# Low parts of the second FFN matrix by an accumulating DMA, in two groups of a hybrid Conformer / mLSTM step

## What is computed

```
h2 = _rmsnorm(x, g_fn)
gt, up = jnp.split(h2 @ w_fi, 2, axis=-1)
x = x + (jax.nn.silu(gt) * up) @ w_fo
```

## Time and profile before

| | us |
|---|---|
| two runs | 1012.42, 1013.75 |
| their median | 1013.09 |
| span of the profiled execution, first to last instruction | 1012.8 |
| TensorE busy in it | 978.7 |
| VectorE, ScalarE, GpSimd busy | 595.8, 382.2, 185.8 |

### The profile page before, as it was taken

How to read it: one execution, slowest core, us unless ns; L and a number is a source line. 1 busy time by engine, 2 the same in 40 slices (tenths; PEclk the granted TensorE clock), 3 DMA queues, 4 the chain that set the end, 5 groups by cost and what they waited for, 6 DMA issues and landing times.

```text
span 1012.8 us, 19204 instructions
## 1 busy us (share of the span) xinstructions
PE 978.7 (97%) x7178; PEld 957.5 (95%) x7178; DVE 595.8 (59%) x870; ACT 382.2 (38%) x511; POOL 185.8 (18%) x160
## 2 busy tenths in 40 slices
PE   6999989999999999999999999999999999999993
PEld 5999879999999999999999999999999999999993
DVE  6876768698597869875365553333333343333355
ACT  5643444345235434536533443331122221122242
POOL 4042051014005101400230022220022220022202
PEclk9989989999999999999999999999999999999997
DMA  6227403521521352142522222223222222222222
GB/s 188 79 63 147 105 22 116 188 83 42 218 84 42 124 177 83 42 139 81 177 84 76 85 86 81 77 77 99 83 72 88 89 86 83 83 82 78 66 64 93
DMA packets 29389, 96.96 MB, mean 96 GB/s; under 512 B 7296, under 2 KB 7440, under 8 KB 28320
## 3 DMA queue, kind: packets, MB, share of 16 engines
q1 hardware_dynamic: 27600, 78.01, 24.5%
q0 software_dynamic: 1744, 18.42, 5.8%
HBM read 84.03 MB, written 12.39 MB: 95 GB/s over the span
## 4 chain that ended last, share of the span: by engine, by line
PE 51%; issue 32%; DVE 5%; POOL 5%; ACT 4%; DMA 2%; POOLq 0%; SPq 0%; DVEq 0%; ACTq 0%
PE ps L892 38%; POOL hf L587 3%; PE ps L1137 3%; PE ps L992 2%; POOL hid_lo L589 2%; DMA raw<-w_head_in 2%; ACT hid_hi L869 2%; PE ps L1016 1%; PE ps L1064 1%; PE ps L1002 1%; DVE w_lo L1170 1%; PE ps L1073 1%; DVE rs L1185 1%; DVE hf L1232 1%; ACT w_hi L614 1%
## 5 line engine op out<-in xcount | busy, mean ns | idle before, releaser
L892 PE MATMUL ps<-h_hi,w_hi 128*128 128x288 f32 x1472 | 317.0, 297 | 1.4 <-DVE w_lo L1170 1.4
L892 PE MATMUL ps<-h_lo,w_hi 128*128 128x288 f32 x1472 | 314.4, 295 | 0.0
L892 PE MATMUL ps<-h_hi,w_lo 128*128 128x288 f32 x1472 | 314.4, 295 | 0.0
L614 ACT ACTIVATE w_hi<-raw 128x1024 fp32r<-128x1024 f32 x136 | 143.8, 1058 | 383.1 <-PE ps L892 370.6
L1170 DVE TENSOR_TENSOR w_lo<-raw,w_hi 128x1024 fp32r<-128x1024 f32 x136 | 191.4, 1408 | 160.2 <-ACT w_hi L614 159.5
L892 PEld LDWEIGHTS ps<-h_hi,w_hi 128*128 128x128 f32 x1472 | 236.1, 189 | 3.3 <-issue 2.6
L892 PEld LDWEIGHTS ps<-h_lo,w_hi 128*128 128x128 f32 x1472 | 237.0, 189 | 0.0
L892 PEld LDWEIGHTS ps<-h_hi,w_lo 128*128 128x128 f32 x1472 | 236.9, 189 | 0.0
L1385 DVE SCALAR_TENSOR_TENSOR conv<-a_p,vec,conv x120 | 96.8, 807 | 0.2
L587 POOL TENSOR_TENSOR hf<-hf,rs 128x576 f32<-128x576 f32 x22 | 31.4, 1426 | 347.8 <-DVE hf L1609 347.8
L1575 DVE TENSOR_TENSOR x<-ps,x 128x576 f32 (+1 forms) x32 | 24.3, 758 | 89.8 <-PE ps L892 89.8
(11 more groups left out here) (255 smaller groups left out, 1223.8 us busy)
## 6 DMA issues: line engine op xcount, KB each, us to landing
raw<-w_fi_in SPq DMA_DIRECT2D x44, 512.0 KB, 3.5
raw<-w_head_in SPq DMA_DIRECT2D x40, 512.0 KB, 3.5
cs<-st_c_in POOLq DMA_DIRECT2D x4, 2048.0 KB, 9.2
c_s_out<-cs POOLq DMA_DIRECT2D x4, 2048.0 KB, 7.7
raw<-w_fo_in SPq DMA_DIRECT2D x16, 512.0 KB, 3.5
x<-xT_in SPq DMA_DIRECT2D x16, 288.0 KB, 4.1
raw<-w_cgcv_in SPq DMA_DIRECT2D x8, 512.0 KB, 3.7
raw<-w_ga_in SPq DMA_DIRECT2D x8, 512.0 KB, 3.5
```

The costliest lines, as they stand in the source:

```text
L614: act.activation(w_hi[:, s, :], raw[:, s, :], ACT.Copy).then_inc(hi_ready, 1)
L892: last = pe.matmul(ps[:, 2 * s + b, 0:HALF], wt[:, w, k * P:k * P + P], src[:, k, b * HALF:b * HALF + HALF], start=(k == 0 and wt is w_hi ...
```

## The change

In groups 0 and 1 of the FFN, for the eight splits made in the loop of the second matrix, the subtraction on DVE goes. ACT writes the negated rounded weight into `w_lo[s]` right behind the rounded one (`-raw`, written as `F32R`, is rounded like `raw`). POOL then issues a DMA that adds the raw weight onto it, with `accum_op=ALU.add`, which leaves raw minus rounded. In group 0 the DMA reads the raw weight from the buffer `raw[s]` in SBUF, in group 1 from the weights in DRAM again. DVE waits until the DMA has landed (`lo_landed[s]`) and raises `lo_ready` itself, twice through the same order: first its own wait that the previous increments are there, then the increment. There are 16 such splits of the kernel's 136. All others stay as they were.

```diff
@@ gpsimd, behind the loop over hidden tiles of group g
+                def add_raw(at, s, of):
+
+                    pool.wait_ge(neg_ready, at + (s + 1))
+                    pool.dma_start(w_lo[:, s, :], of, accum_op=ALU.add).then_inc(lo_landed[s], 16)
+
+                for n in range(KT if g < 2 else 0):
+                    beyond = n + 2 - KT
+                    if g == 0:
+                        of = raw[:, n % 2, :]
+                    else:
+                        of = w_fo1[n + 2] if beyond < 0 else w_fi[2 * Q_E[2] + beyond]
+                    add_raw(g * KT + n - n % 2, n % 2, of)
@@ scalar, the loop of the second matrix
                             split_hi(i + (U_F[g] + 2) // 2, s)
+                            act.activation(w_lo[:, s, :], raw[:, s, :], ACT.Copy, scale=-1.0).then_inc(neg_ready, 1)
@@ vector, add_units
-                    if not last:
+                    if base in U_F[:2]:
+
+                        dve.wait_ge(lo_landed[s], i * 16 + (8 * KT * U_F.index(base) + 16))
+                        dve.wait_ge(lo_ready, i * 2 + (base + s + 2))
+                        dve.sem_inc(lo_ready, 1)
+                    elif not last:
                         split_lo(i * 2 + (base + s + 2), s)
```

More of the change, by code:

```diff
@@ L325, in build @@
         lo_ready = sem("lo_ready")
+        neg_ready = sem("negated_hi_ready")
+        lo_landed = [sem(f"lo_landed{s}") for s in range(2)]
         unit_done = sem("unit_done")
```

## The result

The changed kernel took 1035.75 us (two runs, 1032.79 and 1038.71) against 1013.09: ratio 1.0215, interval 1.0183 to 1.0247. Four more runs of the same file, on another occasion, gave 1030.81 against 1014.8, ratio 1.0155, interval 1.0131 to 1.0179. So it is slower, by 2.2% in the first set and by 1.6% in the second. The forecast was 1031, the range 1015 to 1060. The execution profiled first is the slower of the two: 1038.7 us, span 1036.8, 24.0 us over the span of before.

What follows compares the result with a forecast made beforehand. TensorE was taken to bound the kernel; 8 stalls of 1.85 us (14.8) plus 3.2 us contention made 18 us on the 1012.8 us span, 1030.8, plus 0.3 to the median: 1031 us. Range 1015 to 1060.

Steps and rivals of the forecast that it cites:

- what bounds: Second matrix of group 0: TensorE sets the pace, busy the whole stretch; removing 19.6 us of DVE subtractions saves nothing.
- the sign: Whole kernel: slower, by 1.8%; chance of being faster 0.02.
- the budget: Second matrices: TensorE wants a unit's low part 6.07 us after its rounding starts; the new chain takes 7.9 us.
- The hops: Chain to the low part: 0.3 us for POOL's pick-up, 0.3 us for landing to DVE and DVE to PE.
- ACT's pair of instructions: Chain to the low part: rounding then negated copy on ACT, 1.06 us each, 2.12 us; the extra work is hidden.
- A: Adding DMA from issue to landing, issuing time included: 5.2 us taken, lower bound 3.1, upper bound 9.2.
- the doubling: Adding DMA: fetching two rows adds a second 1.4 to 1.8 us, giving 4.5 to 5.3 us.
- one stop for two units: Second matrices of groups 0 and 1: one stall per two units, 8 for 16 splits, 1.85 us each, 14.8 us.
- Contention: Adds with next raw loads in flight: 0.4 us more per landing, 8 x 0.4 = 3.2 us.
- Clock: TensorE's clock after stalls: a stall of 2.2 us loses no clock, so nothing is in the sum.
- Rival 2: Adding DMA well below half rate: landing from 5.9 us, 20.4 to 47 us cost, clock up to 24 more; chance 0.34.
- rival 1: Adding DMA's two reads overlap fully: landing 3.1 to 3.3 us, nothing changes, 1013 us; chance 0.12.

Runs made afterwards that it cites:

- The last one: Against the kernel before: adds of both groups from SBUF, low weights last in units served by adds and first matrices of groups 1 and 2; 1016.64 us, ratio 1.0011.
- the control of one of them: The kernel before with TensorE's products reordered to high x high, high x low, low x high from group 0's second matrix on, no adding DMA; 1030.87 us, ratio 1.0159.

## Why the prediction was right, and where not

**Right: what bounds, and the sign.** TensorE sets the pace, the work taken off DVE is worth nothing, the negated copies are free. The kernel in which DVE adds shows the third (0.999). The last one shows the second: DVE has only its additions to `x` in S0, 6.06 us, and the time is that of before.

**Right: the budget.** 6.07 us from the start of a rounding until TensorE wants the low part. A copy with 2.9 us stays inside and stops nothing, one with 3.9 us stops a little, the add with 4.5 stops it 0.7 to 0.9 us as the profile shows it and costs 1.1 to 1.2. The hops (0.31 for POOL, 0.37 for the two others) came out nearly as read from the rows of before; ACT's pair of instructions took 2.01 instead of 2.12, since the second starts 0.97 after the first.

**Wrong in size: A, and that it was one number.** 5.2 us was taken. Measured: 4.5 from SBUF, 5.2 to 8.0 from DRAM. The prediction knew that the source changes between the groups and priced both alike, although the rows it stood on were of both kinds (a store out of SBUF and a load from DRAM). In place of 1.85 us a stop costs 4.6 / 4 = 1.15 in group 0; in group 1 TensorE stood still for up to 2.5. The prediction itself named landings that differ by far between the two sources as a sign of being wrong, and that sign came, as did one of its slow rival, landings over 6 us with a clock below 1.00, in group 1 of the first profile. For SBUF the doubling from the row of the store, 1.7 + 2 x 1.4 = 4.5, gives the measured 4.5, though the plain copy in it took 2.9 and not 3.1; the upper end was chosen because of the load's row, which is DRAM's. The Trainium skill's two pages (DMA: Bandwidth & Descriptors, Anatomy of one DMA; Collectives: The Full Stack, The bandwidth ceiling) gave 4.4 as an estimate, by the fixed 2.0 us and a doubled data part; the second says it of the add in a ReduceScatter between cores. The traces are near it for SBUF: 2.9 for the copy, where the first page gives 3.2, and 4.5 for the add. For DRAM, where 3.9 and 5.6 were measured, they fall short by 0.7 and 1.2 us, and the measurement decides.

**Half right: one stop for two units.** In group 0 there are four stops for eight splits, as derived. In group 1 nearly every unit stopped (six and eight stops for eight splits in the two profiles of the changed kernel, 15 for 16 in the kernel with both from DRAM). The derivation took A as equal for the two units of a pair. It isn't: the load for the next unit is released when TensorE starts again, and from then on an add and a load from DRAM are under way together. Where all adds of group 1 had a load beside them and landed within 6.5 to 7.1 us, in the kernel with the early load, there were four stops for the eight again. The cost hardly depends on the count: each chain starts at the end of the unit two before, so two stops in a row share one lateness. By the prediction's own sum with the measured landing, a pair costs 2.72 + 4.5 - 6.07 = 1.15 us, 4.6 for group 0 (measured 4.6), and 2.72 + 5.6 - 6.07 = 2.25 from DRAM, 9.0 for group 1 (measured 8.2 in the second profile, in which no clock was lost).

**Contention.** Estimated at 0.4 us for all. Measured 0 to 0.3 in group 0 of the changed kernel, 1 us and more in group 1 with the early load (6.6 against 5.2 to 5.6 for an add that meets no load).

**Clock: not in the sum, and not always nothing.** The prediction took stops of 2.2 us as free of clock loss. In the first profile of the changed kernel they were not. Windows around its stops of 2.05 and of 2.45 us (columns as in the earlier trace rows):

```profile
857.90:860.20 2.30, 0.28 (x3) 0.04 (x1) 0.00 (x0) 1.98 (x2) 0.00 (x0) 1.00 0.05 9
860.20:868.40 8.20, 8.17 (x50) 8.17 (x51) 0.76 (x1) 0.02 (x1) 0.85 (x1) 0.79 0.62 132
...
876.30:883.00 6.70, 6.61 (x48) 6.38 (x48) 0.76 (x1) 0.47 (x1) 0.85 (x1) 1.00 0.70 144
883.00:885.40 2.40, 0.01 (x1) 0.04 (x1) 0.09 (x1) 2.00 (x2) 0.06 (x1) 1.00 0.17 34
885.40:893.50 8.10, 8.10 (x50) 8.10 (x51) 0.67 (x1) 0.00 (x0) 0.79 (x1) 0.79 0.66 131
```

The unit behind each took 8.2 and 8.1 us instead of 6.3, at a mean clock of 0.79: 8.2 + 8.1 - 2 x 6.33 = 3.6 us that the sum hadn't. Stops of 1.94 and 1.61 us in the same group were followed by units at 1.00, but in the kernel with both adds from DRAM the units behind stops of 1.85 and 1.78 us ran at 0.79 (its lines are above). So the length of the stop alone doesn't decide: between 1.78 and 1.94 us both happened, and no stop of up to 1.6 us was followed by a lower clock in these stretches. In the second profile no stop was above 1.6 and no clock was lost, which fits 3.6 of the 5.8 us between 64.8 and 59.0 in S1.

**Not seen at all: the pace of the untouched loop.** 2.4 to 2.6 us in E1; the prediction had the rest of the kernel unchanged.

**The sum.** 18 us were forecast as 8 x 1.85 + 3.2. The second profile has 16.4: 4.6 in S0, 2.6 in E1, 8.2 in S1, 0.8 in E2, 0.2 for all else. The first has 24.0: 4.6, 2.4, 14.0, 1.3 and 1.7. That 18 lies between them is partly luck. The prediction's price for each group was 4 x (1.85 + 0.4) = 9.0 us. That is twice what group 0 took; in group 1 it is near the second profile (8.2) and too low for the first (14.0); and E1's pace filled a gap. Rival 2 (a slow add) named the right mechanism for the extra in group 1, long landings and lost clock, but for all sixteen, where only eight had it; rival 1 (hidden) is what a copy does in group 0.

## What to carry to other kernels

Before moving an elementwise step from an idle engine into a DMA, write down the budget from the release of its buffer to its use, and add up the chain with one landing price per kind of source; an add costs about half as much again as a copy of the same bytes. If the chain is longer than the budget, the remedy that worked here is to have the consumer ask later: running the products that don't need the late operand first hid 16 DMAs of 4.5 to 7.4 us, as far as the times show, while what then becomes late (the reload of the same buffer, an operand that the new order wants earlier) has to be checked with it. Count stops of TensorE of some 1.8 us and more at a higher price than their length: here the clock fell after most of them, for some 1.8 us more each.

## What the runs showed of the hardware that was not expected

- Adding a 512 KB tile onto SBUF by DMA: 4.5 us from SBUF, 5.2 to 5.6 from DRAM alone, and up to 8.1 beside a load; the plain copies 2.9 and 3.9. POOL spends 0.85 us per issue of an add, and 0.53 on a plain copy of the same bytes.
- An add from SBUF is not immune to loads: among those of group 0, 4.5 to 4.9 us where TensorE stopped and an add had a load beside it for 2.1 us at most, and up to 7.4 where TensorE didn't stop and the two overlapped for up to 4.8.
- The same loop over the first matrix of a group runs at one of two paces, 12.48 or 12.80 us per pair of units, at a granted clock of 1.00 in both. TensorE doesn't stand still in either: at 12.48 the matmuls start 128 to 132 ns apart; at 12.80 three in four come after 130 to 132 ns and every fourth after 140. Before had 12.48 in group 1 and 12.80 in group 2. Group 1 went to 12.80 in every kernel with stops inside S0, with DMAs or without, but also in two of those with the low weights last, where TensorE stopped ahead of S0 and not in it; the control of one of them, with the same stop ahead, kept 12.48. And group 2 ran at 12.80 behind a second matrix without stops in the kernel before, and at 12.48 in the kernels with the DMA in group 0 alone and with the slow DVE. What sets the pace is open; it is worth 2.6 us here in group 1 and 1.8 in group 2, and makes effects of 0.2% hard to read from a single change.
